# Expert weights of a mixture-of-experts layer: gate and up loaded, awaited and freed in two halves of the contraction

## The reference, cut to what matters

```
# 64 experts, two per token; w_gate, w_up: (64, 1024, 512), w_down: (64, 512, 1024)
hid = silu(x_block @ w_gate[e]) * (x_block @ w_up[e])
y_block = hid @ w_down[e]
```

## Time and profile before

| | us |
|---|---|
| median of three runs | 5243.85 |
| the profiled execution, its time | 5262.38 |
| its span, first to last instruction | 5260.8 |
| first gate product of the experts' stage | 3761.7 |
| last gate product of that stage | 5111.2 |
| TensorE waiting for gate and up weights in the stage | 87.9, in 32 waits |

### The profile page before, as it was taken

One profiled execution on the slowest core, in us unless ns is written; L12 is line 12 of the kernel. 1 busy time (PEld: TensorE's weight loads), 2 busy tenths in 40 slices (PEclk: granted clock), 3 DMA queues, 4 the chain that ended last, 5 costly groups with the idle time before them and its releaser, 6 DMA issues. The chain is left out here.

```text
span 5260.8 us, 122702 instructions
## 1 busy us (share of the span) xinstructions
PE 4374.7 (83%) x47298; PEld 2979.5 (57%) x47298; DVE 2214.8 (42%) x4008; ACT 1249.5 (24%) x3133; POOL 1565.5 (30%) x1949
## 2 busy tenths in 40 slices
PE   3998799989968988888888886788499999988990
PEld 1877676666648777777877775444133333333330
DVE  1112166666645454554544544888211111111118
ACT  0001044344423333333323332332000000000002
POOL 0000001001025464554545543443322222221224
PEclk7999999999989999999999988888699999999995
DMA  9311165556442223232232324442675888899766
GB/s 310 124 59 68 58 198 186 166 173 197 150 128 68 77 71 91 71 78 68 71 91 71 89 57 122 144 138 97 232 299 209 341 350 341 362 373 400 316 265 263
DMA packets 365528, 916.96 MB, mean 174 GB/s; under 512 B 181136, under 2 KB 220432, under 8 KB 332080
## 3 DMA queue, kind: packets, MB, share of 16 engines
q1 hardware_dynamic: 310224, 759.97, 41.4%
q0 software_dynamic: 47392, 133.02, 7.2%
q10 hardware_dynamic: 7488, 17.83, 0.9%
HBM read 951.09 MB, written 211.26 MB: 221 GB/s over the span
## 5 line engine op out<-in xcount | busy, mean ns | idle before, releaser
L2410 PE MATMUL exp_gate_up<-exp_w_gate,exp_rows_and_rowsT 128*64 128x512 f32 x1664 | 768.2, 620 | 88.8 <-DMA exp_w_up<-in_moe_w_up_dram 87.9
L2410 PE MATMUL exp_gate_up<-exp_w_up,exp_rows_and_rowsT 128*64 128x512 f32 x1664 | 768.9, 621 | 0.0
L2410 PEld LDWEIGHTS exp_gate_up<-exp_w_gate,exp_rows_and_rowsT 128*64 128x64 f32 x1664 | 234.9, 143 | 588.6 <-issue 588.6
L1544 POOL TENSOR_TENSOR rw_A_level<-rw_A_rho_beta,const_level_masks 128x256 f32<-128x256 f32 x432 | 338.2, 799 | 706.6 <-DVE rw_A_rho_beta L1560 440.0
L721 PE MATMUL rwp_product<-rwp_hT,rwp_w_rw 128*128 128x256 f32 (+1 forms) x2016 | 445.0, 384 | 0.0
L874 PE MATMUL hgp_product<-hgp_hT,const_w_hg 128*128 128x256 f32 x1728 | 411.1, 394 | 26.5 <-DMA hgp_hT<-s_hT 15.7
L2362 DVE TENSOR_TENSOR exp_hidden<-exp_hidden,exp_gate_up 64x512 f32<-64x512 f32 x104 | 71.9, 692 | 821.4 <-ACT exp_hidden L2343 821.4
L721 PEld LDWEIGHTS rwp_product<-rwp_hT,rwp_w_rw 128*128 128x128 f32 (+1 forms) x2016 | 381.7, 190 | 61.6
L874 PEld LDWEIGHTS hgp_product<-hgp_hT,const_w_hg 128*128 128x128 f32 x1728 | 338.0, 199 | 87.9 <-DMA hgp_hT<-s_hT 16.1
L2434 PE MATMUL exp_down<-exp_w_down,exp_hiddenT 128*64 128x512 f32 x1664 | 380.0, 598 | 1.1
L1575 DVE TENSOR_TENSOR rw_inverse<-rw_inverse,rw_inverse_bank 128x512 f32<-128x512 f32 x288 | 195.8, 684 | 349.6 <-PE rw_inverse_bank L1454 347.6
(11 more groups left out here) (384 smaller groups left out, 7977.6 us busy)
## 6 DMA issues: line engine op xcount, KB each, us to landing
exp_w_gate<-in_moe_w_gate_dram SPq DMA_DIRECT2D x104, 2048.0 KB
exp_w_up<-in_moe_w_up_dram SPq DMA_DIRECT2D x104, 2048.0 KB
exp_w_down<-in_moe_w_down_dram SPq DMA_DIRECT2D x104, 2048.0 KB
s_rw_in<-prep_operands SPq DMA_DIRECT2D x72, 514.0 KB, 4.0
rw_operands<-s_rw_in SPq DMA_DIRECT2D x72, 514.0 KB, 5.6
rw_tokens<-s_rw_tm SPq DMA_DIRECT2D x144, 192.0 KB, 6.5
hg_qkf<-s_hg_in SPq DMA_DIRECT2D x36, 768.0 KB, 7.9
mod_w<-in_w_mod_dram SPq DMA_DIRECT2D x24, 1024.0 KB, 26.1
```

The lines of the kernel that those rows point to most:

```text
L1544: nc.gpsimd.tensor_tensor(self.al[d][l % 2][:], self.ar[u][d][:, :, 0, :], self.K["lvc"][:, d, l, :].unsqueeze(1).broadcast_to([P, NPAIR, ...
L2410: i = nc.tensor.matmul(pgu[u][q:q + BLK], xT[:, k, r * BLK:(r + 1) * BLK], w[r][:, k, :], start=(k == 0), stop=(k == KD - 1))
```

## The change

Gate and up weights have two semaphores per lane instead of one, for k 0 to 3 and for k 4 to 7, and each matrix is loaded by two DMAs of 1 MB, each of which takes 8 KB per partition. SyncE issues the first halves of gate and up after `gate_up_half`, a new semaphore that TensorE raises with the last product of k = 3, and the second halves after `gate_up_done`. TensorE waits for the first halves before k = 0 and for the second halves before k = 4. The SyncE function `load` now only reads the registers, and it stands ahead of the waits: once per lane for gate and up, once per lane for down. The down weights are still one DMA of 2 MB per lane.

```diff
@@ -2249,10 +2249,12 @@
-        names = ("gate_up_done down_done ...
+        names = ("gate_up_half gate_up_done down_done ...
-        gate_up_loaded, down_loaded = ([m.sem(f"{x}_loaded{r}") for r in range(LANES)] for x in ("gate_up", "down"))
+        down_loaded = [m.sem(f"down_loaded{r}") for r in range(LANES)]
+        gate_up_loaded = [[m.sem(f"gate_up_loaded{r}{h}") for h in range(2)] for r in range(LANES)]
+        KH = KD // 2
@@ -2266,25 +2268,27 @@
-                def load(g, r, which, done):
+                def load(g, r):
                     e = sp.value_load(K["block"][0:1, 0, bass.ds(g * LANES + r, 1)], min_val=0, max_val=N_EXP - 1)
                     skip = {}
                     if not isinstance(g, int):
                         skip = {"cond": sp.value_load(K["block"][0:1, 1, bass.ds(g * LANES + r, 1)], min_val=0, max_val=1)}
-                    for w, buf in which:
-                        sp.dma_start(buf[r][:], A[w][0, bass.ds(e, 1)].rearrange("o (p k) f -> p (o k) f", p=P), **skip).then_inc(done[r], 16)
+                    return e, skip
 
                 def body(g):
                     for u in range(2):
-                        wait(sp, s["gate_up_done"], 2 * (g - 1) + u + 1)
-                        sp.sem_inc(s["turns"], 1)
-                        for r in range(u * SUB, (u + 1) * SUB):
-                            load(g, r, (("moe_w_gate", wg), ("moe_w_up", wu)), gate_up_loaded)
+                        e, skip = load(g, u)
+                        for h, free in enumerate(("gate_up_half", "gate_up_done")):
+                            wait(sp, s[free], 2 * (g - 1) + u + 1)
+                            sp.sem_inc(s["turns"], 1)
+                            for w, buf in (("moe_w_gate", wg), ("moe_w_up", wu)):
+                                src = A[w][0, bass.ds(e, 1)].rearrange("o (p k) f -> p (o k) f", p=P)
+                                sp.dma_start(buf[u][:, h * KH:(h + 1) * KH, :], src[:, h * KH:(h + 1) * KH, :], **skip).then_inc(gate_up_loaded[u][h], 16)
                     for u in range(2):
+                        e, skip = load(g, u)
                         wait(sp, s["down_done"], 2 * (g - 1) + u + 1)
                         sp.sem_inc(s["turns"], 1)
-                        for r in range(u * SUB, (u + 1) * SUB):
-                            load(g, r, (("moe_w_down", wd),), down_loaded)
+                        sp.dma_start(wd[u][:], A["moe_w_down"][0, bass.ds(e, 1)].rearrange("o (p k) f -> p (o k) f", p=P), **skip).then_inc(down_loaded[u], 16)
@@ -2400,16 +2404,18 @@
-                    for r in lanes:
-                        pe.wait_ge(gate_up_loaded[r], 32 * g + 32)
-                    pe.sem_inc(s["turns"], 1)
                     for k in range(KD):
+                        if k % KH == 0:
+                            for r in lanes:
+                                pe.wait_ge(gate_up_loaded[r][k // KH], 32 * g + 32)
+                            pe.sem_inc(s["turns"], 1)
                         for c, w in ((0, wg), (64, wu)):
                             ...
-                    i.then_inc(s["gate_up_done"], 1)
+                        if k % KH == KH - 1:
+                            i.then_inc(s[("gate_up_half", "gate_up_done")[k // KH]], 1)
```

More of the change, by code:

```diff
@@ L2251, in experts @@
         ph = m.ps("hidden_turned", [P, KF, 64])
-        names = ("gate_up_done down_done x_turned xT_ready silu_ready hid_ready h_turned hT_ready out_ready turns tok_loaded rows_loaded "
+        names = ("gate_up_half gate_up_done down_done x_turned xT_ready silu_ready hid_ready h_turned hT_ready out_ready turns tok_loaded rows_loaded "
                  "slot_loaded0 slot_loaded1 stored0 stored1 gate_loaded").split()
         s = {n: m.sem(n) for n in names}
-        gate_up_loaded, down_loaded = ([m.sem(f"{x}_loaded{r}") for r in range(LANES)] for x in ("gate_up", "down"))
+        down_loaded = [m.sem(f"down_loaded{r}") for r in range(LANES)]
+        gate_up_loaded = [[m.sem(f"gate_up_loaded{r}{h}") for h in range(2)] for r in range(LANES)]
+        KH = KD // 2
         def steps(eng, body):
```

## The result

The changed kernel takes 5166.42 us, the median of four runs (5161.71 to 5170.17), against 5243.45 for the kernel before, here of four runs too. The medians differ by 77 us. The ratio on record, which isn't the quotient of the two medians, is 0.9843 with a 95% interval of 0.9808 to 0.9879, a gain of 63 to 101 us. 5173 was predicted, with a range of 5130 to 5208. The profiled execution takes 5170.17 us and has a span of 5168.6, 92 us less than before.

The account below looks back on a forecast made before the run. Late gate and up weights, loaded in bunches into single buffers, cost some 134 us; 45 + 9 + 8 = 62 remain, 71 to 72 go. Profiled 5262.4 becomes 5191, less 18.5 gives median 5173, range 5130 to 5208.

Parts of the forecast that it names:

- Loads come in bunches, and a bunch's time sets the loss: Experts' stage: loaded lanes come bunched; time from first possible issue to last due date sets the loss, some 134 us.
- The registers, 1.4 us sooner: SyncE's register loads and arithmetic go ahead of its wait, so loads issue 1.4 us sooner (bounds 0.54 and 1.7).
- Freed 3.4 us sooner, awaited 3.4 us later: Gate and up loads: first half issued 3.4 us sooner, last half due 3.4 us later; with registers, 8.4 us per bunch.
- the first rival: TensorE waits before k = 4 instead, so only the early start counts: about 45 us gained, 5199; chance 0.10.
- A half costs 0.05 us more, 9 us: Each queued 1 MB gate or up load in bunches costs 0.05 us more; 184 halves, 9 us.
- The slower rival: In SyncE's queue in bunches, 1 MB loads are dear: at 3.3 us each, 67 us slower, 5311; chance 0.05.
- What remains: Experts' stage after the change: 45 us shortage, 9 for halves, 8 for clock; 62 of 134 us remain.
- the four lone pairs: Bunches of a two-lane step then a one-lane step, not joined to others after the change: short by 1.0 us each.
- the scale of 0.9: Factor on summed bunch shortages, since they gave 148 us before the change against 134 measured; turns 49 into 45 after.
- The clock: Experts' stage: granted clock rises to 0.98 or 0.99; about five long waits still pull it down, 1.7 us each, 8 us.
- The waits left over sit in the two long bunches: Remaining gate-weight waits, 25 to 50 us instead of 87.9, sit in 4500 to 4800 us, in the two long bunches.
- Nearly all waits go: Experts' stage: clock stays up, all but the longest bunch's 24 us goes; 110 us gained, 5134; chance 0.10.

Follow-up runs that it names:

- single-part kernels: Against the kernel before: registers read early alone, 0.9965; registers early plus halves freed early but awaited whole, 0.9909; registers early plus halves awaited separately but freed whole, 0.9940.

## Why the prediction was right, and where its numbers were off

- *Loads come in bunches, and a bunch's time sets the loss.* Right. The single-part kernels lose 124.8, 91.4 and 97.5 where the whole change loses 52.4.
- *The registers, 1.4 us sooner.* 1.5 by the timeline. Worth 12 us alone and 13 at the end, each by the loss in one trace.
- *Freed 3.4 us sooner, awaited 3.4 us later.* Both real and of like worth, 36 and 30 us, and 9 more together. The wait in the middle, the first rival, exists in the trace but doesn't take the gain away.
- *A half costs 0.05 us more, 9 us.* Too much: 2.2 us in all, 0.01 each. This is the first mis-sized term. The slower rival had its price from a lone 1 MB load, 4.2 us; queued halves run at 421 GB/s. The Trainium skill (DMA: Bandwidth & Descriptors, Bandwidth) has 6.15 us and 341 GB/s for 1 MB, measured on loads that GpSimd issues. The traces disagree for SyncE's loads that queue behind each other. The prediction's estimate from it, 660 us, rests on the 6.15 us; at the 341 GB/s of the same row a half would take 3.1 us, and the estimate would be about 100 us. Nor is the rule of the Trainium skill (the same section), at least 1 MiB for each DMA, against the change, as the prediction had it: a half is 1024 KB, just 1 MiB.
- *What remains.* The sum had 45 of shortage, 9 for the halves and 8 for the clock, 62, and 3 in the first step. Measured are 52.4. By the starts of the steps in TensorE's timeline the four lone pairs lose 2.4 together (4 forecast, unscaled), the joined bunch of steps 16 to 18 0.3 (1), the two of six lanes 6.1 and 5.2 (4.9 each), the one of 32 to 34 13.8 (10.6), and the longest 23.2 (24); the first step 1.3. Without the scale of 0.9, the halves and the clock, these five groups are 49 forecast and 51 measured. The scale belonged to the kernel before: by the same reading the ten pairs lost 88 us there, the two single steps 6, the bunches of 5 and of 7 lanes 16 and 24, against 94, 6, 19 and 29 forecast. (The 3 us of a single step don't come from the formula as it is written, which gives 15. They come if one counts to lane 1's products, 6.8 us later, with no down load due.) That 49 meets 51 is luck in part. With the 421 GB/s of full stretches in place of 412 the same sums give 133 before, against the 134 of the trace without any scale, but only 35 after. The other 16 us behind the change no run takes apart.
- *The clock.* 0.99, at the upper end of the 0.98 to 0.99 forecast. As a term of 8 us on top of the shortage it wasn't needed: in the longest bunch a step of 32.37 us is accounted for by its bytes at 421 GB/s, with a granted clock of 0.95 in it.
- *The waits left over sit in the two long bunches.* Mostly: 37 of the 52 us.
- *The median.* 71 of gain were forecast; the stage gave 84, the medians 77. The step that was off is the sum of what remains, 65 with the first step against 52.4, so 13 us too much, of which 7 are the halves' cost. That the median came within 7 us of 5173 is luck in part. The profiled execution was forecast at 5191 and took 5170, 21 less: 13 from the stage and 8 from its earlier start, where nothing was changed. And the 18.5 us by which it was to lie above the median were 3.8.
- *Nearly all waits go*, the second rival, had 24 us left, where the stage still loses 52. Its gain of 110 us lies outside the interval of 63 to 101. It is out, as is the first rival's 45.

## What to carry to other kernels

With single-buffered weights that come in bunches, the gain of a finer buffer is read from two moments: how much sooner a bunch may begin, and how much later its last piece is due; both count (36 and 30 us here) until the bunch's bytes at the full rate of the DMA engines are all that is left. Then finer pieces give nothing: check the busiest stretch for its share and its GB/s before cutting further. And where an engine issues behind a wait, look at what stands between the wait and the issue: register reads of 1.5 us moved ahead of it were worth 12 us of the stage here.

## What the runs showed that I had not expected

With the registers read early the list of waits didn't shrink (89.5 us against 87.9) while 12 us were gained, and the gate products' busy time fell by 13.6. The 9 us that the two ends bring only together came out of TensorE's busy time as well. My reading, which no run tests by itself: in a stretch that the DMA engines pace, TensorE's slow products use up time that would otherwise be listed as waiting.

A step without waits took 23.43 us in the kernel without down loads (4002.00 less 3978.57, lane 0's silu), against 23.52 in all others. Two things differ there on TensorE: the wait for down weights compares with a constant and not with a value worked out from the loop's register, and it was met long ago. Which of them saves the 0.05 us per lane wasn't tried.
